# Ten-sublayer fp32 transformer on one core: operand halves at unequal distances from the weights modulo 256 bytes, with matmuls and vector work at the sublayers' seams in another order

## The reference, cut to what matters

```python
x = x + 0.5 * gate(0) * _swiglu(norm_mod(x, 0), w_ffn_up[l, 0], w_ffn_down[l, 0])
x = x + gate(1) * _mixer(norm_mod(x, 1), w_in[l], ...)
x = x + 0.5 * gate(2) * _swiglu(norm_mod(x, 2), w_ffn_up[l, 1], w_ffn_down[l, 1])
...
mix = group_rmsnorm(jnp.concatenate([y_a, y_b, y_c, y_d], axis=-1), g_group[l])
x = x + gt1 * (mix @ w_out[l])
h = rmsnorm(x, g_ffn[l]) * (1.0 + sc2) + sh2
f = (jax.nn.silu(h @ ffn_w1[l]) * (h @ ffn_w3[l])) @ ffn_w2[l]
x = x + gt2 * f
```

## Time and profile before

| | us |
|---|---|
| three executions | 1657.39, 1661.45, 1661.53 (median 1661.45) |
| the profiled execution's own time | 1664.79 |
| its span, first to last instruction | 1663.0 |
| TensorE busy | 1599.3 (96%) |
| TensorE loading weights | 1573.3 (95%) |
| VectorE busy | 1312.3 (79%) |
| ScalarE busy | 914.2 (55%) |
| mean granted TensorE clock | 0.988 of full |

### The profile page before, as it was taken

The page is one execution under the profiler, slowest core; times in us unless marked ns, Lnnn a source line. Parts: engine busy times, 40 slices in busy tenths (PEclk is TensorE's granted clock), DMA queues, the critical chain, the costliest instruction groups (busy, mean ns, idle before and its releaser), DMA issues. The chain is left out here.

```text
span 1663.0 us, 31915 instructions
## 1 busy us (share of the span) xinstructions
PE 1599.3 (96%) x13270; PEld 1573.3 (95%) x13270; DVE 1312.3 (79%) x2071; ACT 914.2 (55%) x1567; POOL 86.7 (5%) x124
## 2 busy tenths in 40 slices
PE   2999999899999999999899999999999999999998
PEld 2999998899999999998899999998999999899998
DVE  6788888688888878888788788878888879786753
ACT  5455459564444645458565545565545456664553
POOL 5000000010000000000030001001000010010000
PEclk8999999999999999999999999999999999999999
DMA  9787764357776787764367877424788863355661
GB/s 356 296 335 311 314 254 151 134 199 306 298 310 273 280 306 294 295 233 153 123 236 299 318 294 280 155 102 178 261 324 302 315 245 127 109 187 202 238 254 52
DMA packets 57168, 403.22 MB, mean 242 GB/s; under 512 B 6606, under 2 KB 6866, under 8 KB 9280
## 3 DMA queue, kind: packets, MB, share of 16 engines
q1 hardware_dynamic: 55424, 396.01, 62.6%
q0 software_dynamic: 1600, 5.18, 1.1%
HBM read 400.10 MB, written 1.05 MB: 241 GB/s over the span
## 5 line engine op out<-in xcount | busy, mean ns | idle before, releaser
L1616 DVE TENSOR_TENSOR WL<-ring,WH 128x1024 fp32r<-128x1024 f32 (+1 forms) x508 | 600.3, 1216 | 193.8 <-ACT WH L1153 193.1
L518 PE MATMUL PS<-HH,WH 128*128 128x256 f32 (+1 forms) x2640 | 637.5, 284 | 16.5 <-ACT WH L1153 10.0
L518 PE MATMUL PS<-HL,WH 128*128 128x256 f32 (+1 forms) x2640 | 625.2, 280 | 0.0
L1153 ACT ACTIVATE WH<-ring 128x1024 fp32r<-128x1024 f32 (+1 forms) x508 | 510.3, 1049 | 102.8 <-DMA ring<-in_down 47.5
L518 PEld LDWEIGHTS PS<-HH,WH 128*128 128x128 f32 x2640 | 496.3, 189 | 23.9 <-ACT WH L1153 9.7
L518 PEld LDWEIGHTS PS<-HL,WH 128*128 128x128 f32 x2640 | 494.9, 190 | 0.8
L518 PE MATMUL PS<-HH,WL 128*128 128x256 f32 (+1 forms) x2640 | 375.8, 281 | 3.5 <-DVE WL L1616 3.5
L518 PEld LDWEIGHTS PS<-HH,WL 128*128 128x128 f32 x2640 | 338.4, 190 | 4.9 <-DVE WL L1616 4.6
L1643 DVE CUSTOM_DVE_ANT_0 ring<-ring,CB,VC 128x1024 f32<-128x1024 f32 x240 | 317.8, 1339 | 9.1 <-DMA ring<-in_ada 9.1
L518 PE MATMUL PS<-AH,WH 128*128 128x256 f32 x1056 | 295.1, 279 | 0.0
L518 PE MATMUL PS<-AH,WL 128*128 128x256 f32 x1056 | 294.8, 279 | 0.0
(11 more groups left out here) (214 smaller groups left out, 1450.0 us busy)
## 6 DMA issues: line engine op xcount, KB each, us to landing
ring<-in_up SPq DMA_DIRECT2D x88, 1024.0 KB, 5.8
ring<-in_ada SPq DMA_DIRECT2D x72, 1024.0 KB, 7.1
ring<-in_ffn SPq DMA_DIRECT2D x66, 1024.0 KB, 5.8
ring<-in_mod SPq DMA_DIRECT2D x48, 1024.0 KB, 6.9
ring<-in_down SPq DMA_DIRECT2D x44, 1024.0 KB, 5.6
ring<-in_win SPq DMA_DIRECT2D x32, 1024.0 KB, 6.9
ring<-in_wout SPq DMA_DIRECT2D x16, 1024.0 KB, 4.8
ring<-in_winv SPq DMA_DIRECT2D x4, 1024.0 KB, 4.9
```

The costliest lines, as they stand in the source:

```text
L518: return e.matmul(out, lhsT, rhs, start=start, stop=stop, skip_group_check=skip)
L1153: e.activation(half_of(i)[0], slot_of(("unit", u))[:, w * (i % 2):w * (i % 2) + w], ACT.Copy).then_inc(s_hi, 1)
L1616: return e.tensor_tensor(out, a, b, op)
```

## The change

1. **Distances.** A table `AT_256` gives each sublayer two offsets, one for HH (and AH), one for HL (and AL). HH, HL, AH and AL become ten tensors each at the same place but for this offset, and WH, WL begin at byte 128 of 256. The distances of the moving operand from its weights, modulo 256 bytes, rounded part and remainder: n = 0 (192, 64), n = 2 (64, 192), n = 3 (192, 128), n = 5 (64, 128), n = 7 (192, 0), n = 9 (64, 0). The mixers keep (192, 192). YH and YL stay 192 bytes past the weights. The scratch behind AL moves by 128 elements.
2. **Entries.** In `cols` with `first` and n > 0, TensorE runs WH·HH and then WL·HH for chunks 0 to 6, then both for chunk 7, then WH·HL.
3. **The end of mix1.** VectorE's `lo(u0 + 12)` is taken apart: its halves now come behind the two diagonals and behind the last `tile_rest`; `stick_tile` comes earlier by one share and those two halves. ScalarE's `hi(u0 + 12)` is taken apart likewise. TensorE turns tiles 2 and 3 over behind chunks 4 and 5 of round 0, one chunk earlier.
4. **The last loop of all mixers.** Slot u0+14 is prepared half by half: ScalarE's second half two chunks later, VectorE's second half behind the loop.
5. **Modulation.** `ADA_N` is 18 in n = 5 and 3 in n = 6, so shares 6 and 7 leave sublayer 6.
6. **The distance bias** is gathered on the host and comes as an input; the matmul, the copy, the write and their waits go, and the constants are 320 columns shorter.

```diff
-ADA_N = (21, 3, 19, 19, 2, 17, 4, 20, 3, 4)
+ADA_N = (21, 3, 19, 19, 2, 18, 3, 20, 3, 4)
...
+AT_256 = ((192, 64), (192, 192), (64, 192), (192, 128), (192, 192), (64, 128), (192, 192), (192, 0), (192, 192), (64, 0))
...
-        HH = sb("HH", [128, KD, 320], F32R)
-        HL = sb("HL", [128, KD, 320], F32R)
-        pad = sb("pad", [128, 16])
+        HHL = []
+        for i, part in enumerate(("HH", "HL")):
+            part_at = nc.sbuf_base
+            sb("room_" + part, [128, KD * 320 + 64])
+            HHL.append([nc.alloc_sbuf_tensor_at(f"{part}{n}", [128, KD, 320], F32R, offset=part_at + AT_256[n][i]) for n in range(NSUB)])
+        HH, HL = HHL
...
-        AH = nc.alloc_sbuf_tensor_at("AH", [128, NF, S], F32R, offset=scr_at)
-        AL = nc.alloc_sbuf_tensor_at("AL", [128, NF, S], F32R, offset=scr_at + 4 * NF * S)
+        AH, AL = ([nc.alloc_sbuf_tensor_at(f"{part}{n}", [128, NF, S], F32R, offset=at + (64 + AT_256[n][i]) % 256) for n in range(NSUB)]
+                  for i, (part, at) in enumerate((("AH", scr_at), ("AL", scr_at + 4 * NF * S + 256))))
...
@@ TensorE, cols @@
                 e.wait_ge(s_hi, i + 1)
...
                 if first:
+
+                    for ks in (range(KD - 1), (KD - 1,)) if n > 0 else (range(KD),):
+                        for k in ks:
+                            e.wait_ge(s_hh, 8 * n + k + 1)
+                            mm(out, wh[:, k, :], HH[n][:, k, 0:S], start=k == 0, stop=False)
+                        e.wait_ge(s_lo, i + 1)
+                        for k in ks:
+                            mm(out, wl[:, k, :], HH[n][:, k, 0:S], start=False, stop=False)
                     for k in range(KD):
                         e.wait_ge(s_hl, 8 * n + k + 1)
...
@@ TensorE, mixer1 @@
-                    5: (lambda: turned_out(n, o0 + 2),),
-                    6: (lambda: turned_out(n, o0 + 3),),
+                    4: (lambda: turned_out(n, o0 + 2),),
+                    5: (lambda: turned_out(n, o0 + 3),),
...
@@ ScalarE, mixer1; the last three lines in mixer2 too @@
-                hi(u0 + 12)
                 tile_scale(n, o0 + 2)
                 tile_scale(n, o0 + 3)
+                hi_half(2 * u0 + 24)
                 tile_out(n, o0 + 2)
+                hi_half(2 * u0 + 25)
                 tile_out(n, o0 + 3)
...
-                    if c == 3:
-                        hi(u0 + 14)
+                    if c in (3, 5):
+                        hi_half(2 * u0 + 28 + (c - 3) // 2)
...
@@ VectorE, the last loop of both mixers @@
-                        lo(u0 + 14)
+                        lo_half(2 * u0 + 28)
                     if c > 0:
                         gained(n + 1, c - 1)
                 gained(n + 1, KD - 1)
+                lo_half(2 * u0 + 29)
```

More of the change, by code:

```diff
@@ L523, in cols @@
                 e.wait_ge(s_hi, i + 1)
[L524 to L532, removed]
-                if first:
+                if first:
+                    for ks in (range(KD - 1), (KD - 1,)) if n > 0 else (range(KD),):
[5 more added lines that the diff above has]
+                            mm(out, wl[:, k, :], HH[n][:, k, 0:S], start=False, stop=False)
                     for k in range(KD):
                         e.wait_ge(s_hl, 8 * n + k + 1)
-                        last = mm(out, wh[:, k, :], HL[:, k, 0:S], start=False, stop=k == KD - 1)
+                        last = mm(out, wh[:, k, :], HL[n][:, k, 0:S], start=False, stop=k == KD - 1)
+                else:
+                    for k in range(KD):
+                        mm(out, wh[:, k, :], HH[n][:, k, 0:S], start=k == 0, stop=False)
+                        mm(out, wh[:, k, :], HL[n][:, k, 0:S], start=False, stop=False)
+                    e.wait_ge(s_lo, i + 1)
+                    for k in range(KD):
+                        last = mm(out, wl[:, k, :], HH[n][:, k, 0:S], start=False, stop=k == KD - 1)
                 last.then_inc(s_half, 1)
@@ L601, in tokens @@
                         for k in range(4):
-                            mm(out, HH[:, 4 * i + k, q], wh[:, k, :], start=i == 0 and t == 0 and k == 0, stop=False, skip=True)
-                            mm(out, HL[:, 4 * i + k, q], wh[:, k, :], start=False, stop=False, skip=True)
+                            mm(out, HH[n][:, 4 * i + k, q], wh[:, k, :], start=i == 0 and t == 0 and k == 0, stop=False, skip=True)
+                            mm(out, HL[n][:, 4 * i + k, q], wh[:, k, :], start=False, stop=False, skip=True)
                     e.wait_ge(s_lo, h + 1)
@@ L607, in tokens @@
                         for k in range(4):
-                            last = mm(out, HH[:, 4 * i + k, q], wl[:, k, :], start=False, stop=i == 1 and k == 3, skip=True)
+                            last = mm(out, HH[n][:, 4 * i + k, q], wl[:, k, :], start=False, stop=i == 1 and k == 3, skip=True)
                     last.then_inc(s_half, 1)
@@ L1577, in _ @@
                 e.activation(SQ[:, c, :], xr, ACT.Identity, bias=shift, scale=gain).then_inc(s_xn, 1)
-                e.activation(HH[:, c, 0:S], xr, ACT.Identity, bias=shift, scale=gain).then_inc(s_hh, 1)
+                e.activation(HH[0][:, c, 0:S], xr, ACT.Identity, bias=shift, scale=gain).then_inc(s_hh, 1)
                 if c == 5:
```

110 lines of the change are left out of this document (47 added, 63 removed).

## The result

The changed kernel takes 1665.99 us (median of 10 runs, 1663.25 to 1666.94); the kernel before, on the same chip between them, 1659.42 (10 runs, 1650.07 to 1678.29). The ratio is 1.0048, 95% interval 1.0027 to 1.0069: **slower** by half a percent, where I forecast 1645.3 and gave "slower" 0.18. The ratio leaves out the one slow execution of the kernel before, 1678.29. The profiled execution took 1666.64 us.

A forecast was written before the change was run, and what follows sets the result against it. TensorE, busy 96% of the span, was taken to bound the kernel by matmul rate and stops. Terms -3.2 - 4.5 - 2.0 - 2.6 - 0.6 - 3.3 = -16.2 took 1661.45 to 1645.3 us; range 1622 to 1680.

The forecast's parts named there:

- The end of mix1: Sublayers 1 and 4: TensorE's 3.70 us idle goes as copies no longer wait behind a WL half; -3.2 and -4.5 us.
- the last loop: End of each of four mixers: one WL half moves behind the loop, shortening VectorE's chain; -0.5 us each, -2.0 in all.
- the bias: Distance bias from the host: two matmuls at 835.88 to 836.51 go; -0.6 us.
- modulation: Sublayer 6 loses shares 6 and 7, which sublayer 5's VectorE slack covers; -2.6 us.
- The entries: Nine sublayer entries: seven matmuls reading WL cover the 0.37 us wait for the last HH chunks; -3.3 us in all.
- The lower clock: Behind mix1's TensorE wait, granted clock 0.57 over 8 us; some of that time counted as gained within sublayer 4's -4.5 us.
- The seams together: Sum of all terms, from mix1's end, last loops, modulation, bias and entries: -16.2 us.
- The distances: Feed-forward matmuls at unequal distances: sublayers fall on the two levels again, about half and half; 0, bounds -52 to +48 us.
- all slow: Rival: every feed-forward sublayer falls to 0.1173 us a matmul; +18.1 us, so 1663.4; chance 0.10.
- some pairs collide on every matmul: Rival: in feed-forward sublayers some distance pairs wait each time, step towards 0.1206 us; at most +48, 1693 us; chance 0.18.
- break-even: Mean feed-forward matmul step from which colliding distances outweigh the -16.2 us gain: 117.1 ns, against 115.3.
- The rule of two read ports: TensorE loads next weights without taking bandwidth from the running matmul, so placement is worth nothing, as in the sum.

The follow-up runs named there:

- 9: Kernel before, plus 30 matmuls of 256 columns with four columns of weights in the feed-forward sublayers, results overwritten: 1650.17 us.
- run 8: Changed kernel with all distances back at (192, 192), plus 30 overwritten matmuls with four columns of weights: 1633.84 us, ratio 0.9857 to the kernel before.
- the streams: Kernels of back-to-back 256-column matmuls alone, computing nothing of the reference, at chosen distances, orders or weight widths: 113.3 to 120.1 ns a matmul with full weights.
- 6: Changed kernel with all distances back at (192, 192), run once more unchanged for a second trace: 1639.47 us.
- 7: Kernel before, run once more unchanged for a second trace: 1657.42 us.
- the seams alone: Changed kernel with all distances set back to (192, 192), its other changes kept: 1644.51 us, ratio 0.9887 to the kernel before.
- 11: As run 8, but with the last chunk's two matmuls of an entry back ahead of the seven that read WL: 1637.36 us.

## Why the prediction was wrong, point by point

- **The end of mix1**, -3.2 and -4.5 us: right in direction; sublayer 4 was taken too large. Stretches 1 and 4, which hold also the last loop (-0.5 each) and an entry (-0.37), came down by 4.4 and 3.9 us where these terms give 4.1 and, with the bias, 6.0. In sublayer 1 VectorE does set the end, as forecast: TensorE's 3.70 us fell to 0.57, and 1.74 came back for X. (The copies moved ahead of the two WL halves alone; the share ahead of them stayed there.)
- **The last loop and modulation**, -2.0 and -2.6: stretches 6 and 8 gave 4.3 and 1.6 where the terms with the entry give 3.5 and 0.9. The 2.23 us wait kept 1.03.
- **The entries**, -3.3: mis-sized a little. 28.65 - 26.03 = -2.6 us; the two-part loop leaves 1.96 us for 16 matmuls that need 16 x 0.1173 = 1.88 at the slow level.
- **The lower clock**, which I priced in sublayer 4 alone. TensorE's waits of over 0.15 us at the four mixers' ends add up to 17.2 us before and 11.1 in the changed kernel, 6.1 less, though the mixers gave 14.2. Entries and bias give some 1.7 of the rest. The other 6 us or so, an estimate, go with the clock: where it was low, matmuls of 256 columns started every 0.213 us (321.35, 321.56, 321.77 and so on in the trace before), against 0.113 to 0.118. By the same account nearly all of it lies in sublayers 1, 4 and 6. No run holds the clock apart from the waits. So a good part of the seams' gain is not the waits that I subtracted but what the clock did behind them, and that the sum came out is in part luck.
- **The seams together**, -16.2: runs 9 and 8 differ by 16.3. Next to nothing of the error lies here.
- **The distances**, 0: this is the step that failed. "Both levels occur at both distances that the trace has, so I expect the six sublayers to fall on the two levels again, about half and half." Both levels do occur at an equal 192, but none of the six pairs has the quick one: the streams give 115.6 to 118.6, the changed kernel 117.4 to 118.4 by sublayer. The term was put at nothing because two levels had been seen, with no row at any of the pairs. Its six means average 117.8 against my 115.3, and 2.5 ns x 9024 is 22.6 us: 1645.3 + 22.6 = 1667.9, 2 us from the 1666.0 measured. What misled me was `tokens`: with the roles swapped, moving 64 bytes past the weights, 24 matmuls in a row did come every 113 ns. The streams at (64, 64) never did, so a row from swapped roles doesn't speak for this product; why it differs was not tried.
- **Of the rivals**, "all slow" (1663.4, chance 0.10) came nearest in time, but by the mechanism of "some pairs collide on every matmul" in a mild form. Its break-even, 117.1 ns, was the right yardstick: 117.8 lies beyond it. I gave both too little because I took the two levels of one trace for properties of the sublayers. One more trace of the kernel before would have shown that they are draws (runs 6 and 7), and that a change of placement puts every quick draw at stake: 4220 of the matmuls in that trace could only lose.
- **The rule of two read ports**, from the Trainium skill (TensorE: Matmul & The Clock Gate, Step-by-step), says that loading the next weights takes no read bandwidth from the running matmul. The streams disagree with what I drew from it, that placement is worth nothing: beside a full load a matmul takes 120.0 ns at (0, 0) and 113.3 at (192, 192), and at (0, 0) it takes 113.3 beside a load of four columns. (That form also writes only four rows of PSUM, which no run keeps apart from the load; the step from distance 0 to 192 doesn't hang on it.) The measurement decides. The 109.2 ns that I worked out from the Trainium skill's formula (same page, Back-to-back issue gap), an estimate, was met by no 256-column stream in any run; 113.3 was the least. The Trainium skill calls it there the gap of an isolated matmul, and I had read it as one for a stream.

## What to carry to other kernels

When a stretch that is nothing but back-to-back matmuls shows two rates in one trace, take a second trace of the same kernel before giving the rates a cause: a rate drawn at each wait is neither a property of the place nor of the code, and it hides or fakes changes of 1% in the time. When a change removes waits, compare the granted clock behind them too: it can be worth as much as the waits. Where a layout puts an operand relative to its weights is worth a table of measured streams (four of 9 us a pair) before it is worth an edit. And a change of many parts should be timed in two: here the reordering gained 16 us, one table lost some 22, and their sum looked like next to nothing.

## What the runs showed of the hardware that I had not expected

- A matmul of 256 columns with a full load beside it comes every 113.3 or every 117.8 ns when it reads 192 bytes past its weights modulo 256, and in the streams never at 113.3 at any of the fifteen other pairs of 0, 64, 128 and 192, or at equal 32, 96, 160 and 224 (115.6 to 120.1). Weights began at byte 192 in the kernel before, 128 in the seams alone and 0 in the streams, and 192 past them both rates were there each time.
- The two rates are two phases. They last over 100 us, through changes of bank and of weights, and can end at waits (0.64 us was enough, and once a stop of 0.1 us) or at a matmul of another kind. In the streams one of 256 columns with four columns of weights, at 113 ns, left the quick one each time (five times from quick, once from slow), one at distance 64 the slow one. In the kernel such a four-column matmul left the slow one in runs 8 and 11 at about 42 us, where the clock was at the lower level or just coming up (0.66 over 41:42 in run 8).
- Unequal distances cost 2.6 to 3.6 ns a matmul even with four-column weights. Why, and why 192 is the good distance, stays open: no run here tells what in the memory the two streams share. In the changed kernel the same pair, (192, 0), costs 119.3 ns in the down projection and 116.1 in the up projection; that too stays open.
